# Latent attention with norms by tokens, keys' shared part rotated once, and the output divided with queries on partitions

## The chip, the cores and the metric

The kernel is one program on one core of a Trainium2 chip. The time is device microseconds of one execution, and a kernel's time is the median of several. A profile is one further execution with the hardware profiler on. PE is the TensorEngine, ACT the ScalarEngine, DVE the VectorEngine, POOL GpSimd; SP only issues transfers.

## The reference, cut to what matters

The whole computes two transformer blocks of two layers each. The change lies in one stage, the latent attention (MLA) of the first block's first layer, over 256 context and 512 latent tokens (768, kept as 512 latent and then 256 context), in float32:

```python
def mla_heads(z, q_norm_g, w_uq, kv_norm_g, w_ukv, qn_g, kn_g, ang):
    cq, ckv, kr = z[..., :256], z[..., 256:384], z[..., 384:]      # 256, 128, 32 wide
    q = (rmsnorm(cq, q_norm_g) @ w_uq).reshape(b, t, 8, 96)
    kv = (rmsnorm(ckv, kv_norm_g) @ w_ukv).reshape(b, t, 8, 64 + 64)
    k = concatenate([kv[..., :64], broadcast(kr, 8 heads)], axis=-1)
    v = kv[..., 64:]
    q, k = rmsnorm(q, qn_g), rmsnorm(k, kn_g)                      # over the 96 of each head
    if ang is not None:                                            # latent tokens only
        q = concatenate([q[..., :64], apply_rotary(q[..., 64:], ang)], axis=-1)
        k = concatenate([k[..., :64], apply_rotary(k[..., 64:], ang)], axis=-1)
    return q, k, v

p = softmax(q @ k.T * 96 ** -0.5)      # latent queries: all 768 keys; context queries: context keys
out = p @ v
```

`rmsnorm(x, g)` is `x * rsqrt(mean(x * x) + 1e-6) * g`. After it come a retention over the same input, an output projection and the rest of the network.

## The kernel before, in words

Every engine runs its own program in order, and semaphores tie them together. `PLAN_TICKETS` deals PSUM's eight banks out to the steps in program order: PE claims a ticket's bank (`claim`: it must have been drained the time before), fills it (`fill`), and a reader waits (`filled`) and drains it (`drained`); `emptied` waits for a ticket's drain. `PLAN_BLOCKS` deals the slots of `ring`, which holds weights, and says after which ticket a slot may be loaded anew. SP issues all weight loads in one fixed order, each behind the wait for its slot: `w_in0`, `uq`, `ukv`, twelve `ada_w` halves, four `w_in` blocks for the retention, then, with no wait, 40 copies of later weights (`weights_kept`, `gate_weights`), then `w_out`.

Activations lie with channels on partitions and the 768 tokens along the free side, in two parts of 512 and 256 (`TBS`).

**The stem.** PE multiplies `w_in0` by the input (`z_kv`, `z_q0`, `z_q1`, `z_kr`, L2800). ACT squares and copies each bank; PE sums squares over channels by a product with a matrix of ones (L812), which gives each sum on all partitions; ACT takes roots, DVE inverts 128x512 and 128x256 of them (L855) and scales `cqT` and `ckvT` (L856). `v_tok` holds the values of all heads with tokens on partitions, one product of 128x512 for each of six token tiles (L2810).

**The loop.** `mla_order` yields (step, number) for PE, ACT and DVE alike. Step number n from 0 to 47 is head n // 6 and query tile n % 6; four tiles are latent (768 keys), two are context (256 keys). Steps for n: `scores` n (L2859), `scale` n-1, `turn` n-2 (L2865), `out` n-3 (L2874). DVE takes the maximum (L2072, one for each bank), ACT the exponential with its sum (L1614), DVE divides the probabilities by the sum (L2085), PE turns them so that keys are on partitions, DVE and ACT copy the turned tiles (L2091, L1626), and PE multiplies `v_tok` (64 columns of weights) by them (128 moving columns), with the result as 64 channels x 128 queries; DVE copies it to `mixT` (L2095).

In between, the next head is prepared: `proj` (query L2831 and key L2836 projections, each copied and squared by ACT, the shared `krT` again for each head, L1590 to L1597), `nsum` (ones-products of queries and keys, L2843, and on ACT `Identity`, `Ln` and later `Exp` and `Square`, L824 to L833), `norm` (DVE: a Newton step, L840, L841, and the scaling, L2054) and `rot` (product with the rotation matrix, L2850, and three DVE operations on 32 partitions, L2062 to L2065), the last three for queries and keys apart. `ada`, `adarow`, `adacol` make a piece of the modulation vectors for later layers, one per head (L731, L738, L745). `stay_awake` (L799) issues products of the identity whose result nobody reads.

Names: `qh`, `kh` are the queries and keys of a head (two buffers), `prob_of` three buffers of probabilities, `probT` two of turned ones, `stat` small columns, P = 128, NL = 512, NC = 256, NT = 768, QK = 96, NOPE = 64, H_A = 8.

## Time and profile before

| | us |
|---|---|
| median of 3 runs (lowest, highest) | 3968.12 (3956.37, 3973.16) |
| the profiled execution | 3971.91 |
| its span | 3969.8 |
| PE busy | 3438.6 (87%) |
| DVE busy | 2098.2 (53%) |
| POOL busy | 1103.5 (28%) |
| ACT busy | 1010.4 (25%) |
| mean granted TensorE clock | 0.943 of full speed |

Times are from the span's start. In the stretches below the attention's stem runs from 45.42 to 127.90 us, its loop from 127.90 to 404.60. A busy share is a mean over stages; in a stage, what PE waits for and how its groups follow one another says what a change is worth there. A float32 matmul appears as two records, a transpose as one. The distance between two groups' starts is their pace; the durations of neighbouring groups overlap a little.

### The profile page before, as it was taken

What the parts mean: (1) busy time and instruction counts of PE and PEld (TensorE: products, weight loads), DVE (VectorE), ACT (ScalarE), POOL (GpSimd) and SP (SyncE); (2) the same over time, 40 slices, a digit from 0 to 9 for tenths busy, and PEclk for the clock granted to TensorE, in tenths of its full rate; (3) what the DMA queues carried; (4) which work ended last, traced back from release to release, by engine and by line L of the source; (5) the groups of instructions that cost most, each with busy time, mean ns of one, the idle gap of its engine ahead of it and who ended that gap; (6) DMA issues with size and microseconds to landing.
All of it is one profiled execution on the core that took longest, in us unless ns stands there. A gap on an engine that the chain in (4) does not pass through costs nothing.

```text
span 3969.8 us, 47914 instructions
## 1 busy us (share of the span) xinstructions
PE 3438.6 (87%) x17905; PEld 2225.1 (56%) x17905; DVE 2098.2 (53%) x4783; ACT 1010.4 (25%) x2338; POOL 1103.5 (28%) x1281
## 2 busy tenths in 40 slices
PE   7888999999999989999999999988677897655655
PEld 4555554555555568788878887765454554211111
DVE  3667036462222258511254246788788445666764
ACT  3665114300000032210162221115432222112212
POOL 0000000254322200000000026654746663333332
PEclk9998999999999999999999999999888999877788
DMA  5325993998787324589521349998969999999998
GB/s 199 128 98 177 330 333 98 255 324 274 219 249 232 120 111 160 189 292 361 181 105 65 128 179 406 412 408 331 332 203 370 388 383 387 421 421 391 422 421 344
DMA packets 337280, 1076.52 MB, mean 271 GB/s; under 512 B 22728, under 2 KB 101012, under 8 KB 292148
## 3 DMA queue, kind: packets, MB, share of 16 engines
q1 hardware_dynamic: 222688, 508.04, 37.5%
q0 software_dynamic: 113968, 565.16, 36.3%
q8 instruction: 126, 2.06, 0.2%
q14 instruction: 78, 0.64, 0.0%
q10 hardware_dynamic: 420, 0.62, 0.0%
HBM read 1045.43 MB, written 236.98 MB: 323 GB/s over the span
## 4 chain that ended last, share of the span: by engine, by line
PE 60%; DVE 17%; DMA 10%; ACT 6%; issue 4%; POOL 2%; another core or an unknown queue 1%; SPq 0%; DVEq 0%; ACTq 0%; POOLq 0%
PE bank L973 22%; PE bank L3169 7%; DMA arena<-expert_rows,arena 5%; PE bank L3395 4%; DVE ring L2708 3%; PE bank L2902 3%; PE bank L3136 3%; DMA ring<-expert_rows,arena 3%; DMA arena<-in_peer_v,arena 2%; PE bank L2968 2%; DVE arena L2708 1%; PE bank L3099 1%; DVE arena L2602 1%; PE bank L2800 1%
## 5 line engine op out<-in xcount | busy, mean ns | idle before, releaser
L3395 PE MATMUL bank<-arena 64*64 64x512 f32 x2520 | 391.3, 697 | 149.9 <-ACT arena L2002 120.5
L973 PE MATMUL bank<-hT,ring 128*128 128x256 f32 (+1 forms) x1536 | 445.5, 452 | 1.9 <-ACT hT L866 1.9
L973 PE MATMUL bank<-arena,ring 128*128 128x256 f32 (+1 forms) x1536 | 442.1, 450 | 0.0
L973 PEld LDWEIGHTS bank<-hT,ring 128*128 128x128 f32 x1536 | 292.7, 191 | 153.4 <-issue 122.4
L973 PEld LDWEIGHTS bank<-arena,ring 128*128 128x128 f32 x1536 | 291.8, 190 | 148.9 <-issue 121.5
L3169 PE MATMUL bank<-hT,ring 128*128 128x256 f32 x1536 | 358.8, 391 | 12.2 <-DVE hT L2424 6.3
L3395 PE MATMUL bank<-ring,arena 64*64 64x512 f32 x1256 | 235.0, 775 | 147.3 <-ACT arena L2002 144.3
L1489 POOL DMA_INDIRECT ring<-in_peer_u,arena x256 | 277.5, 1084 | 220.0 <-DVE ring L2708 106.3
L3169 PEld LDWEIGHTS bank<-hT,ring 128*128 128x128 f32 x1536 | 295.5, 196 | 76.7 <-issue 34.0
L2708 DVE SCALAR_TENSOR_TENSOR ring<-ring,xT 128x1024 f32<-128x1024 f32 x256 | 309.2, 1220 | 30.9 <-DMA ring<-in_peer_u,arena 27.5
L1531 POOL DMA_INDIRECT arena<-in_peer_v,arena x240 | 268.7, 1120 | 181.0 <-issue 59.7
L3395 PEld LDWEIGHTS bank<-arena 64*64 64x64 f32 x2520 | 99.6, 149 | 361.4 <-ACT arena L2002 171.4
L2002 ACT ACTIVATE arena<-arena,rstd 128x64 f32<-128x64 f32 x472 | 141.3, 339 | 423.5 <-DVE rstd L2754 380.5
L2708 DVE SCALAR_TENSOR_TENSOR ring<-ring,bank 128x1024 f32<-128x1024 f32 x141 | 171.8, 1220 | 103.6 <-DMA ring<-expert_rows,arena 99.5
L985 ACT ACTIVATE arena<-bank 128x512 f32<-128x512 f32 (+1 forms) x96 | 43.6, 455 | 713.9 <-PE bank L973 713.9
L1005 DVE SCALAR_TENSOR_TENSOR xT<-bank,modT,xT 128x512 f32<-128x512 f32 (+1 forms) x96 | 54.7, 572 | 317.4 <-PE bank L973 317.3
L3395 PEld LDWEIGHTS bank<-ring,arena 64*64 64x64 f32 x1256 | 57.3, 160 | 290.1 <-ACT arena L2002 220.5
L997 DVE TENSOR_TENSOR arena<-arena 128x512 f32<-128x512 f32 (+1 forms) x96 | 55.9, 590 | 278.6 <-ACT arena L985 277.9
L1508 POOL DMA_INDIRECT ring<-expert_rows,arena x141 | 133.9, 949 | 241.4 <-PE bank L3395 211.6
L785 POOL TENSOR_TENSOR hT<-hT 128x256 f32<-128x256 f32 (+1 forms) x30 | 34.7, 1156 | 582.5 <-ACT hT L1907 261.1
L2708 DVE SCALAR_TENSOR_TENSOR arena<-arena,bank 128x1024 f32<-128x1024 f32 x115 | 140.1, 1220 | 76.1 <-DMA arena<-expert_rows,arena 74.7
L1508 POOL DMA_INDIRECT arena<-expert_rows,arena x115 | 109.0, 948 | 170.9 <-PE bank L3395 149.0
(572 smaller groups left out, 5594.9 us busy)
## 6 DMA issues: line engine op xcount, KB each, us to landing
expert_rows<-in_peer_u SPq DMA_DIRECT2D x32, 2048.0 KB, 20.4
expert_rows<-in_peer_v SPq DMA_DIRECT2D x32, 2048.0 KB, 21.7
ring<-in_mlp_w SPq DMA_DIRECT2D x32, 2048.0 KB, 10.9
ring<-in_ada_w SPq DMA_DIRECT2D x24, 2048.0 KB, 10.5
late_weights<-in_mlp_w SPq DMA_DIRECT2D x32, 1024.0 KB, 14.3
ring<-late_weights SPq DMA_DIRECT2D x32, 1024.0 KB
ring<-weights_kept SPq DMA_DIRECT2D x32, 1024.0 KB
s_store<-arena POOLq DMA_DIRECT2D x8, 2816.0 KB, 9.8
```

The lines of the kernel that those rows point to most:

```text
L973: last = pe.matmul(bank[:, 0:hi - lo], w[:, k, m * P:(m + 1) * P], x[:, k, lo:hi], start=(k == 0), stop=(k == 7))
L997: dve.tensor_tensor(hid[:, m, lo:hi], hid[:, m, lo:hi], hid[:, m, lo:hi], ALU.mult)\
L1489: pool.indirect_dma_start(u_row[u % ERING], None, I["peer_u_2"][0], bass.IndirectOffsetOnAxis(idxs[:, u // EXPERTS, u % EXPERTS:u % EXPERT ...
L1508: pool.indirect_dma_start(both_rows[i % F_SLOTS], None, expert_rows, bass.IndirectOffsetOnAxis(idxs[:, u // EXPERTS, u % EXPERTS:u % EXPER ...
L1531: pool.indirect_dma_start(v_row[v_slot(v)], None, I["peer_v_2"][0], bass.IndirectOffsetOnAxis(idxs[:, v // EXPERTS, v % EXPERTS:v % EXPERT ...
L2002: act.activation(diag[:, d % V_SLOTS, :], eye2, ACT.Copy, scale=acts[:, d % (AGROUP * ACT_GROUPS):d % (AGROUP * ACT_GROUPS) + 1]).then_inc ...
L2708: dve.scalar_tensor_tensor(row, row, 1.0, h_tok[u // EXPERTS], ALU.mult, ALU.mult, accum_out=dots[:, u % 64:u % 64 + 1]).then_inc(S("u_use ...
L2902: last = pe.matmul(bank[:, 0:hi - lo], w[:, k, m * P:(m + 1) * P], hT[:, k, lo:hi], start=(k == 0), stop=(k == KD - 1))
L2968: last = pe.matmul(bank[:, 0:hi - lo], w[:, k, m * P:(m + 1) * P], mixT[:, k, lo:hi], start=(k == 0), stop=(k == 7))
L3136: last = pe.matmul(bank[:, 0:HALF], w[:, k, n % 2 * P:n % 2 * P + P], y, start=(k == 0), stop=(k == KD - 1))
L3169: last = pe.matmul(bank[:, first:first + HALF], w[:, k, c:c + P], y, start=(k == 0), stop=(k == KD - 1))
L3395: last = pe.matmul(banks[2 * r + n][QUADS[r if y == 0 else 1 - r], :], diag[QUADS[r], (v + y) % V_SLOTS, :], v_part(v + y)[QUADS[r], 512 * ...
```

## The change

**Norms with tokens on partitions.** The sum of squares of a head's 96 query or 96 key channels is no longer made by ones-products for each head. Before the loop, PE multiplies once more with tokens on partitions: all heads' key parts (`ksq`, six banks of 128x512) and all heads' queries (`qsq`, twelve banks of 128x480 and 128x288). ACT squares them, DVE sums over each head's channels, so that one root of 128x48 holds all heads and tokens. The norms of `cq` and `ckv` go the same way: 12 and 12 products with one column of ones give sums per token (`kvsum`, `qsum`). The gains of `cq` and `ckv` are applied by ACT's copy, before the products. Values are scaled in their copy (`v_tok`).

**Keys.** Their shared 32 channels are rotated once (`krrot`), turned to tokens on partitions (`krtok`), and DVE writes all heads' keys, scaled, into `keys_tok` (`kmul`, two multiplications for each token tile). In the loop a head's keys are six transposes (`kturn`), copied by ACT with the gain.

**Queries** are projected as before, copied with the gain and rotated; they aren't scaled. The root of a query's norm goes into the exponential's scale and the maximum's factor, which are columns with queries on partitions (`q_pos`, `q_neg`).

**Output.** The probabilities are not divided. Turned probabilities are the weights of the output product and 64 channels of `v_tok` move, so that the result has queries on partitions; DVE divides it there into `att_tok` (L2144 of the new kernel), and after two heads six transposes bring it to `mixT` (`mturn`, four times).

**Banks.** `scores` take a pair of banks, 0 and 1 or 2 and 3 by turns, `turn`, `proj`, `kturn` and `mturn` all the pair 4 and 5, `out`, `rot`, `ada` and `adacol` by turns 6 and 7. A pair is read by one instruction of 768 columns. Maxima, exponentials and the copy of the turned tiles, now ACT's alone, are one instruction each. All `stay_awake` in this stage but the first are gone. `uq`'s slot is free after `kturn7`, where it was after a part of `proj7`. Before the retention's products PE now waits for the last `mturn` to be copied.

The core of the diff (removed lines left out where they are told above):

```diff
 def mla_order():
+    yield from (("proj", 0), ("qsq", 0), ("kturn", 0), ("rot", 0), ("ada", 0), ("adarow", 0))
+    for n in range(6 * H_A + 5):
...
-        for lag, step in ((1, "scale"), (2, "turn"), (3, "out")):
+        for lag, step in ((2, "turn"), (3, "out")):
...
+        if n >= 15 and n % 12 == 3:
+            yield "mturn", (n - 15) // 12
...
+        if h < H_A and n % 6 < 3:
+            yield ("proj", "kturn", "rot")[n % 6], h
...
+def mla_tickets():
...
+        if step == "qsq":
+            yield "qsq", 12, (0, 1, 2, 3, 6, 7)
+        elif step == "scores":
+            yield f"scores{n}", 1, (2 * (n % 2),)
+        elif step in ("turn", "proj", "kturn", "mturn"):
+            yield f"{step}{n}", 1, (4,)
+        elif step != "adarow":
+            yield f"{step}{n}", 1, (6 + odd,)
+            odd = 1 - odd
...
+    ("z_kv", 2), ("z_kr", 2),
+    ("ksq", 6), ("kvsum", 1),
+    ("z_q0", 2),
+    ("krrot", 1), ("v_tok", 6),
+    ("z_q1", 2),
+    ("krtok", 1), ("kmul", 6), ("qsum", 1),
+    *mla_tickets(),
...
-    ("uq", 1, lambda j: (f"proj{H_A - 1}", 1), (1,)),
-    ("ukv", 1, lambda j: (f"proj{H_A - 1}", 3), (2,)),
+    ("uq", 1, lambda j: (f"kturn{H_A - 1}", 0), (1,)),
+    ("ukv", 1, lambda j: ("kturn2", 0), (2,)),
...
+        def turn_kept(act, n):
+
+            t = ticket0[f"turn{n}"]
+            filled(act, t)
+            tiles = slice(0, 6) if n % 6 < 4 else slice(4, 6)
+            w = P * (tiles.stop - tiles.start)
+            drained(act.activation(probT[:, n % 2, tiles, :], pair_of(t)[:, 0:w].rearrange("p (t n) -> p t n", n=P), ACT.Copy), t)
...
+                if step == "adarow":
+                    if n:
+                        filled(act, ticket0[f"adacol{n - 1}"])
+                    ada_keep(act, ticket0[f"ada{n}"], ada_rows_mla)
+                    continue
...
+                elif step == "kturn":
+                    filled(act, t0)
+                    drained(act.activation(kh[0:QK, n % 2, :], pair_of(t0)[0:QK, 0:NT], ACT.Copy, scale=small[0:QK, 4:5]), t0)
+                elif step == "scores" or step == "turn" and n >= 6 * H_A - 2:
+                    if step == "scores" and n >= 2:
+                        turn_kept(act, n - 2)
...
                     act.wait_ge(S("score_max"), n + 1)
...
+                    drained(act.activation(prob_of[n % 3][:, keys], pair_of(t0)[:, 0:keys.stop - keys.start], ACT.Exp,
+                                           bias=stat[:, n % 4, 3:4], scale=q_pos[:, 8 * (n % 6) + n // 6:8 * (n % 6) + n // 6 + 1],
+                                           accum_out=stat[:, n % 4, 4:5]), t0)
...
+                elif step == "out":
...
+                    emptied(dve, ticket0[f"scores{n}"])
+                    dve_step(dve, dve.reciprocal(st[:, 6:7], st[:, 4:5]))
                     bank = filled(dve, t0)
+                    drained(dve.tensor_scalar(att_tok[:, h // 2 % 2, n % 6, HEADROWS[h]], bank[:, 0:V_DIM], st[:, 6:7], None, ALU.mult), t0)
...
+            pe.wait_ge(S("kr_rotated"), 1)
+            bank = claim(pe, ticket0["krtok"])
             for t in range(6):
+                last = pe.transpose(bank[:, ROPE * t:ROPE * t + ROPE], krT[NOPE:QK, t * P:(t + 1) * P], ident[NOPE:QK, NOPE:QK])
+            fill(last, ticket0["krtok"])
+            values("kmul", 0)
...
+                elif step == "kturn":
+                    if n == 0:
+                        for t in range(6):
+                            emptied(pe, ticket0["kmul"] + t)
+                    for t in range(6):
+                        last = pe.transpose(pair_of(t0)[0:QK, t * P:(t + 1) * P], keys_tok[t][:, n, :], ident[:, :])
+                    fill(last, t0)
...
                     for t in tiles:
-                        last = pe.matmul(bank[HEADROWS[h], 0:P], v_tok[:, t, h * 64:(h + 1) * 64], probT[:, n % 2, t, :],
+                        last = pe.matmul(bank[:, 0:V_DIM], probT[:, n % 2, t, :], v_tok[:, t, h * V_DIM:(h + 1) * V_DIM],
                                          start=(t == tiles[0]), stop=(t == 5))
                     fill(last, t0)
+            for last in (f"scores{6 * H_A - 2}", f"scores{6 * H_A - 1}", f"mturn{H_A // 2 - 1}"):
+                emptied(pe, ticket0[last])
```

PE in the stem, behind the second pair of input products (line numbers are each kernel's own, `ring` and `arena` are tiles). Before:

```order
L2800 MATMUL bank<-hT,ring 32x512 x8
L2800 MATMUL bank<-hT,ring 32x256 x8
L812 MATMUL bank<-arena,ones 128x512 x2
L812 MATMUL bank<-arena,ones 128x256 x2
L2810 MATMUL bank<-ring,arena 128x512 x6
L799 MATMUL bank<-ident 128x128 x9
L2831 MATMUL bank<-arena,ring 96x512 x2
L2831 MATMUL bank<-arena,ring 96x256 x2
L2836 MATMUL bank<-arena,ring 64x512
L2836 MATMUL bank<-arena,ring 64x256
L799 MATMUL bank<-ident 128x128 x9
L2843 MATMUL bank<-arena,ones 96x512
```

and now:

```order
L2873 MATMUL bank<-arena 32x512
L2845 MATMUL bank<-ring,arena 128x512 x6
L2857 MATMUL bank<-hT,ring 128x512 x8
L2857 MATMUL bank<-hT,ring 128x256 x8
L2878 MATMUL bank<-ident,arena 128x32 x6
L2845 MATMUL bank<-ring,arena 128x512 x6
L2887 MATMUL bank<-ones,arena 128x1 x12
L2915 MATMUL bank<-arena,ring 96x512 x2
L2915 MATMUL bank<-arena,ring 96x256 x2
L2899 MATMUL bank<-ring,arena 128x480 x2
L2899 MATMUL bank<-ring,arena 128x288 x2
```

The sums over channels (L812) are gone; `krrot` (L2873), `v_tok` and `kmul` (both L2845), `krtok` (L2878), `qsum` (L2887), the first `proj` (L2915) and the first banks of `qsq` (L2899) stand there. `ksq` and `kvsum` come ahead of it.

PE in the loop, around the preparation of the third head. Before, from `proj2` on:

```order
L2831 MATMUL bank<-arena,ring 96x512 x2
L2831 MATMUL bank<-arena,ring 96x256 x2
L2836 MATMUL bank<-arena,ring 64x512
L2836 MATMUL bank<-arena,ring 64x256
L2859 MATMUL bank<-arena 128x512
L2859 MATMUL bank<-arena 128x256
L2865 MATMUL bank<-ident,arena 128x128 x2
L2874 MATMUL bank<-arena 64x128 x2
L799 MATMUL bank<-ident 128x128 x3
L2843 MATMUL bank<-arena,ones 96x512
L2843 MATMUL bank<-arena,ones 96x256
L2843 MATMUL bank<-arena,ones 96x512
```

and now, from `proj3` on, where the pattern is full:

```order
L2915 MATMUL bank<-arena,ring 96x512 x2
L2915 MATMUL bank<-arena,ring 96x256 x2
L2934 MATMUL bank<-arena 128x512
L2934 MATMUL bank<-arena 128x256
L2940 MATMUL bank<-ident,arena 128x128 x2
L2951 MATMUL bank<-arena 128x64 x2
L2923 MATMUL bank<-ident,arena 96x128 x4
L2923 MATMUL bank<-ident,ring 96x128 x2
L2934 MATMUL bank<-arena 128x512
L2934 MATMUL bank<-arena 128x256
L2940 MATMUL bank<-ident,arena 128x128 x6
L2951 MATMUL bank<-arena 128x64 x2
```

The key projection, the stay-awake records and the ones-products are gone; the key turn (L2923) follows the output product of the second step, and the output product (L2951) has 64 columns where it had 128.

ACT in the loop, from an exponential on, before (the first rows of a head's norm):

```order
L1614 ACTIVATE arena,stat<-bank,stat 128x256
L824 ACTIVATE arena<-bank,small 96x512
L825 ACT_TABLE_LOAD
L825 ACTIVATE arena<-bank,small 96x512
L824 ACTIVATE arena<-bank,small 96x256
L825 ACTIVATE arena<-bank,small 96x256
L824 ACTIVATE arena<-bank,small 96x512
L825 ACTIVATE arena<-bank,small 96x512
L824 ACTIVATE arena<-bank,small 96x256
L825 ACTIVATE arena<-bank,small 96x256
L829 ACT_TABLE_LOAD
L829 ACTIVATE arena<-arena 96x768
```

and now:

```order
L1652 ACTIVATE arena,stat<-bank,stat,rstd 128x768
L1640 ACTIVATE arena<-bank,small 96x768
L882 ACTIVATE arena<-bank 128x256
L1652 ACTIVATE arena,stat<-bank,stat,rstd 128x768
L1643 ACTIVATE arena<-bank,small 96x768
L882 ACTIVATE arena<-bank 128x768
L1652 ACTIVATE arena,stat<-bank,stat,rstd 128x768
L882 ACTIVATE arena<-bank 128x768
L1652 ACTIVATE arena,stat<-bank,stat,rstd 128x768
```

The table loads and the norm's activations are gone; exponentials (L1652) alternate with copies of turned tiles (L882), with a query copy (L1640) and a key copy (L1643) in between.

## Rows read from the trace of the kernel before

**Rows 1.** Windows: busy time of each engine, granted clock and DMA share by stretch.

```profile
45.42:127.90 82.48, 77.77 (x324) 42.20 (x325) 31.99 (x40) 33.56 (x63) 0.00 (x0) 0.96 0.26 93
127.90:404.60 276.70, 238.93 (x1375) 149.56 (x1375) 191.56 (x471) 169.90 (x396) 0.00 (x0) 0.94 0.40 138
404.60:1423.00 1018.40, 1011.35 (x3235) 573.43 (x3234) 347.85 (x639) 133.69 (x239) 255.84 (x442) 1.00 0.76 240
```

**Rows 2.** Groups by line, the loop, PE's transposes: busy, mean ns | idle before.

```profile
L2865 PE MATMUL bank<-ident,arena 128*128 128x128 f32 x224 | 36.4, 291 | 32.5 <-ACT arena L1614 17.4 <-DVE arena L2085 10.3 <-ACT rstd L738 4.7
```

**Rows 3.** Timeline of PE, stem and first step: start, duration, line, count.

```profile
45.42 22.21 PE L2800 MATMUL bank<-hT,ring 128*128 128x512 f32 x64 [0.55 <-ACT hT L866]
...
68.76 20.92 PE L2800 MATMUL bank<-hT,ring 128*128 128x512 f32 x64
...
92.30 5.31 PE L2810 MATMUL bank<-ring,arena 128*128 128x512 f32 x12
97.44 2.17 PE L799 MATMUL bank<-ident 128*128 128x128 f32 x18
100.51 2.82 PE L2831 MATMUL bank<-arena,ring 128*96 128x512 f32 x8 [0.89 <-DVE arena L856]
103.26 1.50 PE L2836 MATMUL bank<-arena,ring 128*64 128x512 f32 x4
...
107.76 2.82 PE L2843 MATMUL bank<-arena,ones 96*96 96x512 f32 x8 [0.80 <-ACT arena L1597]
110.52 3.63 PE L731 MATMUL bank<-ring,silu_c 128*2 128x256 f32 x64
...
127.90 1.56 PE L2859 MATMUL bank<-arena 96*128 96x512 f32 x4
129.29 0.38 PE L745 MATMUL bank<-ident,rstd 128*128 128x128 f32 x2
```

**Rows 4.** Timeline of PE, the last head.

```profile
373.57 0.59 PE L2859 MATMUL bank<-arena 96*128 96x256 f32 x2
374.00 0.82 PE L2865 MATMUL bank<-ident,arena 128*128 128x128 f32 x6
374.75 1.52 PE L2874 MATMUL bank<-arena 128*64 128x128 f32 x12
376.21 1.10 PE L2850 MATMUL bank<-arena 96*96 96x512 f32 x2
377.14 0.59 PE L2859 MATMUL bank<-arena 96*128 96x256 f32 x2
379.89 1.54 PE L2865 MATMUL bank<-ident,arena 128*128 128x128 f32 x6 [2.15 <-DVE arena L2085]
381.36 2.34 PE L2874 MATMUL bank<-arena 128*64 128x128 f32 x12
```

**Rows 5.** Timeline of PE, a product with eight moving columns.

```profile
1975.34 3.63 PE L3184 MATMUL bank<-blk,hT 128*128 128x8 f32 x32
1978.83 0.46 PE L3169 MATMUL bank<-hT,ring 128*128 128x256 f32 x1
```

**Rows 6.** Groups by line and shape, ACT and DVE in the loop.

```profile
L1614 ACT ACTIVATE arena<-bank,stat 128x256 f32<-128x256 f32 x48 | 22.4, 467 | 66.4 <-DVE stat L2075 66.4
L1614 ACT ACTIVATE arena<-bank,stat 128x512 f32<-128x512 f32 x32 | 21.9, 683 | 40.7 <-DVE stat L2075 40.5
...
L1614 ACT ACTIVATION_READ_ACCUMULATOR arena<-bank,stat 128x1 f32 x80 | 15.6, 194 | 0.0
L833 ACT ACTIVATE arena<-arena 96x768 f32<-96x768 f32 x14 | 11.8, 843 | 0.4
...
L2072 DVE TENSOR_REDUCE stat<-bank 128x1 f32<-128x512 f32 x32 | 22.0, 687 | 53.9 <-PE bank L2859 53.6
```

**Rows 7.** SP's waits, 404.6 to 1423: us in total, times, longest.

```profile
SPq L645 <- PE bank L2968: 115.2, 2, 90.0
```

**Rows 8.** SP's timeline: the copies behind the retention's weight blocks.

```profile
354.41 43.32 SPq L1260 DMA_DIRECT2D weights_kept<-in_w_in  x12
```

367 lines of the change are left out of this document (190 added, 177 removed).

## The prediction

> **What bounds the kernel now.** I read the page first: PE is the busiest engine, and nearly full in all slices up to the middle. So time goes by TensorE's program order, and a stage is worth what it takes there. The table of stretches then gives the attention's two parts [rows 1]: the stem (the products of `w_in0`, the norms and the first head's preparation) from 45.42 to 127.90 us, 82.5 us, and the loop (48 steps, eight heads of six query tiles) from 127.90 to 404.60, 276.7 us, of which PE is busy 238.9 at a mean granted clock of 0.94. The groups by line show who holds it up: nearly all idle time stands before its transposes (L2865), 32.5 us, for ACT's exponential 17.4, for DVE's division of the probabilities 10.3 and for ada's rows 4.7 [rows 2]. ACT is late because a head's norm puts between exponentials four activations of 0.84 us, four of 0.68 and four of 0.47 (as long as the exponentials' two shapes) and two table loads [rows 6], some 10 us.
>
> At full clock the loop's own work can be added up. A matmul is two records. I take the distance from a group's start to the next start, or, where no start follows, the duration less the 0.07 by which groups overlap. From the stem and the first step [rows 3]: latent scores 1.39 us (127.90 to 129.29), a query projection 2.75 (100.51 to 103.26), a key projection 1.43 (its 1.50 less 0.07), a head's ones-products 2.76 (107.76 to 110.52), ada's products 3.56, ada's turn 0.24 with its overlap off, a stay-awake record 0.12. From the last head [rows 4]: context scores 0.43, six transposes 0.75, an output product of 12 records 1.46 or 0.122 a record, a rotation 0.93. With the loop's counts (8 heads of 4 latent and 2 context steps, 6 and 2 tiles each; seven heads prepared; five adas): 32 x 1.39 + 16 x 0.43 = 51.4; 224 transposes x 0.125 = 28.0; 448 output records x 0.122 = 54.5; 7 x 2.75 = 19.3; 7 x 1.43 = 10.0; 7 x 2.76 = 19.3; 14 x 0.93 = 13.0; 42 x 0.12 = 5.1; 5 x 3.56 = 17.8; 6 x 0.24 = 1.4. Together 219.8. Idle is 276.7 - 238.9 = 37.8, so 19.1 us are left for stretches at 1.2 GHz, which follow waits: after the 2.15 us before 379.89, an output product takes 2.34 us in place of 1.52 [rows 4]. A microsecond of waiting thus costs 1.5.
>
> **The loop, part by part.** Gone are the ones-products (19.3), the key projections (10.0), half the rotations (6.5) and the stay-awakes (5.1). Seven key turns of six transposes come in, 7 x 0.75 = 5.3, and four turns of the output, 4 x 0.75 = 3.0. Scores, turns of the probabilities, query projections and ada stay.
>
> The output product swaps its operands: the weights are now 128 columns of `probT`, the moving side 64 columns of values, in as many records (448). By moving columns a record would halve, 0.061. But a product later in the trace has 128 x 128 weights and 8 moving columns, and its 32 records start over 3.49 us, 0.109 each [rows 5]: below some width records get no shorter. The bounds are 0.061 and 0.122; I take 0.109, since that row has the new form's weights: 448 x 0.109 = 48.8, not 54.5.
>
> The Trainium skill, page "TensorE: Matmul & The Clock Gate", section "LDWEIGHTS (loading the stationary operand)", gives a weight load's time as its column count over 1.2, in ns. By it 128 columns cost 107 ns a record whatever streams past, and the swap saves little; the trace agrees (0.109).
>
> New full-clock sum: 51.4 + 28.0 + 48.8 + 19.3 + 5.3 + 6.5 + 3.0 + 17.8 + 1.4 = 181.5 us.
>
> ACT and DVE no longer bound anything. The norm's work on ACT goes, table loads included. For 768 columns I extend the shapes of 512 and 256 [rows 6]: an exponential 0.68 + 0.22 = 0.90 and 0.19 to read its sum, a copy of turned tiles about as long, a maximum 0.69 x 1.5 = 1.03 at most. A head then takes on ACT 4 x 1.09 + 2 x 0.66 for exponentials, 4 x 0.9 + 2 x 0.47 for turned tiles, 2 x 0.9 for query and key and about 1.5 for ada, 13.5 us, and on DVE about 11 (maxima 5, rotation 2, divisions and factors 4). PE has 22.7 (181.5 / 8). The division of probabilities that PE waited for leaves the path: the quotient is formed behind the output product.
>
> What is late next I find by following one head. After the scores of step n, maximum and factor take 1.3 us, and the exponential ends 2.9 us after the scores, because ACT first copies turn n-2. PE needs it only at turn n, two steps of 3.4 us later. Two places don't fit. At n % 6 = 1 the key turn takes the one bank pair that the turns of the probabilities use, and ACT drains it behind an exponential: turn n-1 of the next step waits about 0.7 us, 7 times, 5. And `ada_keep` (1.5 us of ACT) stands behind the exponential of n % 6 = 3, while the output product of the next step wants ada's bank (two banks take turns): about 1.3 us, 5 times, 6.5. The pipe's start costs 2; at its end the last output, its division, the last turn and ACT's copy of it are one chain before `z_rq`, for which PE now waits: 4. Together 17.5 us of waits, and at 0.5 more for the clock, 9. **Loop: 181.5 + 17.5 + 9 = 208 us, 69 less.** Bounds: 160 with output records of 0.061 and no waits; 240 with records of 0.122 and twice the waits.
>
> **The stem.** The two pairs of input products now take 22.1 and 20.8 us [rows 3], 42.9, after the change as before. Added are three sets of six 512-column products, `ksq`, `v_tok` (which was there) and `kmul`, 5.14 each (92.30 to 97.44, [rows 3]): 15.4; the token sums, 48 records at 0.109, 5.2; the keys' rotation 0.93 and its turn 0.75; `qsq`, six token tiles over 768 columns twice, as much as six query projections, 16.5; the first projection 2.75, key turn 0.75, rotation 0.93 and ada 3.56. These are 46.8. Behind each new wait of PE all the rest of its program is queued, so I followed them: the keys' roots are due before `kmul` and `kr_rotated` before its turn, and `z_q0`, `v_tok` and `z_q1`, 27 us, cover both; the queries' roots, about 4 us of DVE and ACT, lie beside turn, rotation and ada (5.2 us). I allow 1 us. First scores at 45.4 + 42.9 + 46.8 + 1 = 136, against 127.9: **8 us more**. Low end 0, if one-column products are cheaper; high end 16, if DVE's six reductions and twelve multiplications show.
>
> **Behind the attention.** From 404.6 to 1423 PE is busy 1011.4 of 1018.4 us [rows 1], and up to 2300 none of its waits names a DMA. The copies of kept weights that SP issues behind the third `w_in` block start at 354.41 [rows 8], 50 us before the loop's end. That block now waits for the last key turn at step 37, some 33 us before the end, so they come 17 us later against PE. SP afterwards waits up to 90 us for PE at one load [rows 7], which swallows 17, and the block itself is wanted only after `z_rq` and `z_rk`. So I let the whole gain through.
>
> **Sum.** 69 - 8 = 61 us. The profiled execution took 3971.91 us (span 3969.8); 3910.9 for its like. The median shown is 3968.12, 3.8 lower: 3907.
>
> **Rivals.**
> Outputs halve: at 0.061 a record the loop loses 21.5 us more. For it: moving columns set the pace of the wide forms here. Against it: the 8-column row. 3907 - 21 = 3886. Chance 0.08.
>
> A faster pipe: the two bank conflicts don't arise and no stretch falls to 1.2 GHz: 11.5 + 9 = 20 us less, 3887. For it: each is near a microsecond by my count; against it: today's pipe waits at just such places. Chance 0.15.
>
> More waits: without stay-awakes and with a single bank pair PE idles as much as now, 37.8 us and 19 for the clock, so the loop is 238 and the time 3907 + 30 = 3937. For it: the last head, with no norm in it, still waits 2.15 us for DVE [rows 4]; against it: that was the division, which goes. Chance 0.12.
>
> Given back later: the 17 us of later copies reach PE. For it: their queue is full from 354 on; against it: the 90 us. 3924. Chance 0.06.
>
> Slower: the single pair for turns and ACT's strict order make each step one chain: scores 1.39, maximum 1.3, exponential 1.1, turn 0.75, copy 0.9, output 1.3, so 6.7 us for a latent and about 3 for a context step. A head is then 4 x 6.7 + 2 x 3 + 8.0 of preparation = 40.8, the loop 326, and the time 3968 + 50 + 8 = 4026. It decides from 33.6 us a head on, (276.7 - 8) / 8. Against it: scores alternate over two bank pairs and run two steps ahead. Chance 0.02.
>
> The forecast itself has 0.57, within 3896 and 3920. For 8 in 10 over all cases I take 3880 to 3940, which holds the first four rivals. A measurement of this kernel tells about 0.5%, 20 us, from no change: faster 0.95 (all but the last rival and the far ends of two others), within 0.5% 0.03, slower 0.02.
>
> **What would show it.** The profile after should have the first scores near 136 us and `z_rq` near 344; no table load on ACT between the first exponential and the loop's end; output records 0.109 apart; under 20 us of waits of PE in the loop, among them the transposes after a key turn and the outputs after ada; a clock above 0.94 there; and the stretches from `z_rq` on as long as before. I am wrong if the loop stays above 240 us, if the stem grows by over 16, or if a later stretch lengthens by over 10.

## The result: 72 us faster, and where the trace shows them

The changed kernel takes 3897.74 us (median of 4 runs, 3896.71 to 3900.24); the kernel before 3970.27 us (median of 4 runs, 3956.37 to 3973.16; the three known ahead of the prediction and one more). The ratio is 0.9825 with a 95% interval of 0.9801 to 0.9849. Forecast were 3907 us within 3880 and 3940, so sign, size and range hold; the time is 9 us below the forecast, the gain 72.5 us where 61 were forecast. The profiled execution took 3898.42 us, with a span of 3895.5.

First the two parts of the attention and the stretch behind them, from the changed kernel's table of stretches. The columns are length, busy time and instruction count of PE, PEld, DVE, ACT and POOL, then granted clock, DMA share and GB/s.

```profile
45.58:138.89 93.31, 93.31 (x349) 48.51 (x349) 28.67 (x58) 30.97 (x59) 0.00 (x0) 0.96 0.10 37
138.89:333.10 194.21, 180.23 (x1305) 129.45 (x1301) 79.47 (x219) 98.32 (x187) 0.00 (x0) 0.99 0.54 190
333.10:1351.50 1018.40, 1011.25 (x3231) 572.18 (x3232) 347.10 (x635) 133.34 (x238) 255.65 (x442) 1.00 0.78 245
```

Against [rows 1] the stem grows from 82.5 to 93.3 us (10.8 more; forecast 8), the loop falls from 276.7 to 194.2 us (82.5 less; forecast 69), and 1018.40 us counted from `z_rq` on still hold the same work: 1011.25 us of PE, where it was 1011.35. To the end of the span it is 3562.4 us, where it was 3565.2; these 2.8 us were not forecast, and no run explains them. In the loop DVE's busy time falls from 191.6 to 79.5 us, ACT's from 169.9 to 98.3, and the granted clock goes from 0.94 to 0.99.

The groups by line show the loop's PE again; they answer to [rows 2]. Columns: busy time, mean ns of one record, and behind the second bar the idle time before them with what ended it.

```profile
L2951 PE MATMUL bank<-arena 128*128 128x64 f32 x448 | 55.9, 271 | 3.8 <-ACT rstd L752 3.6 <-ACT arena L882 0.2
L2940 PE MATMUL bank<-ident,arena 128*128 128x128 f32 x224 | 32.9, 275 | 5.4 <-ACT arena L1643 3.4 <-ACT arena L1657 1.9
```

The transposes of the probabilities (now L2940) had 32.5 us of idle time before them and have 5.4. No row names the exponential (L1652) any more, and the division (L2144) only once, for 0.5 us before the last turn of the output. PE idles 14.0 us in all (194.21 - 180.23), and its waits say for what (total, times, longest):

```profile
PE bank L2951 <- ACT rstd L752: 3.6, 5, 0.8
PE bank L2940 <- ACT arena L1643: 3.4, 7, 1.3
PE bank L745 <- DMA ring<-in_ada_w: 2.5, 1, 2.5
PE bank L2940 <- ACT arena L1657: 1.9, 3, 1.0
PE bank L2981 <- issue: 1.1, 1, 1.1
PE bank L2945 <- DVE arena L2144: 0.5, 1, 0.5
```

The first is `ada_keep` before the next output product, 5 times, the second the drain of the key turn from the shared bank pair, 7 times: both places that the prediction named. The third it did not name. The last head, from PE's timeline, gives the paces of the new forms (start, duration, line, count), beside [rows 4]:

```profile
317.01 1.51 PE L2934 MATMUL bank<-arena 96*128 96x512 f32 x4
318.36 0.82 PE L2940 MATMUL bank<-ident,arena 128*128 128x128 f32 x6
...
322.70 0.65 PE L2934 MATMUL bank<-arena 96*128 96x256 f32 x2
323.19 0.82 PE L2940 MATMUL bank<-ident,arena 128*128 128x128 f32 x6
323.84 1.45 PE L2951 MATMUL bank<-arena 128*128 128x64 f32 x12
325.13 0.65 PE L2934 MATMUL bank<-arena 96*128 96x256 f32 x2
```

From start to start: latent scores 1.35 us (317.01 to 318.36), context scores 0.49, six transposes 0.65, an output product 1.29 for 12 records, 0.1075 each.

The stem, from the same view, beside [rows 3]:

```profile
73.10 0.28 PE L2868 MATMUL bank<-ones,arena 128*128 128x1 f32 x2
...
76.71 12.28 PE L2857 MATMUL bank<-hT,ring 128*128 128x512 f32 x32
88.93 1.04 PE L2873 MATMUL bank<-arena 32*32 32x512 f32 x2
...
111.31 2.73 PE L2887 MATMUL bank<-ones,arena 128*128 128x1 f32 x24
113.90 4.49 PE L2915 MATMUL bank<-arena,ring 128*96 128x512 f32 x8
118.23 15.64 PE L2899 MATMUL bank<-ring,arena 128*128 128x480 f32 x48
133.71 0.60 PE L2923 MATMUL bank<-ident,arena 128*96 128x128 f32 x4
```

PE never waits in the stem (93.31 us busy of 93.31), yet the granted clock is 0.96. The two slow places stand directly behind the two sets of one-column sums: `z_q0` takes 12.2 us (76.71 to 88.93) and the first projection 4.33 us (113.90 to 118.23), for 10.5 and 2.6 at full clock. The granted clock over these two stretches is 0.86 and 0.61, and 1.00 over the stretches between and behind them.

ACT and DVE, groups by line and shape, beside [rows 6]:

```profile
L1652 ACT ACTIVATE arena<-bank,stat,rstd 128x768 f32<-128x768 f32 x32 | 31.6, 989 | 12.1 <-DVE stat L2133 12.1
L882 ACT ACTIVATE arena<-bank 128x768 f32<-128x768 f32 x32 | 25.9, 810 | 53.0 <-PE bank L2940 52.9
L1652 ACT ACTIVATION_READ_ACCUMULATOR arena<-bank,stat,rstd 128x1 f32 x48 | 9.5, 198 | 0.0
...
L1652 ACT ACT_TABLE_LOAD x1 | 1.3, 1283 | 0.0
```

```profile
L2132 DVE TENSOR_REDUCE stat<-bank 128x1 f32<-128x768 f32 x32 | 30.6, 958 | 61.7 <-PE bank L2934 61.7
```

One table load is left, before the first exponential. ACT now waits mostly for PE (53 us before the copies of turned tiles), where it had waited mostly for DVE's maxima (107 us before the exponentials, now 12).

SP's timeline, beside [rows 8], shows the transfers that the prediction followed.

```profile
259.61 40.05 SPq L659 DMA_DIRECT2D ring<-in_w_in  x4
299.70 44.95 SPq L1291 DMA_DIRECT2D weights_kept<-in_w_in  x12
...
544.22 19.75 SPq L659 DMA_DIRECT2D ring<-in_ada_w  x2
633.93 0.37 SPq L659 DMA_DIRECT2D ring<-in_mlp_w  x1
```

The kept copies start 33.4 us before the loop's end (333.10 - 299.70), where they had 50.2. SP still stands still for some 70 us later on (564 to 633.93), so the 17 us are swallowed and nothing is given back.

### The profile page after: what moved, and what is told of

Read it like the earlier page. It is cut to its first block, busy times and chain, and to the rows that moved or that the text cites. A ratio compares the mean times of both kernels' runs of the same rounds, so it can differ in the third digit from the quotient of the medians.

```text
span 3895.5 us, 47385 instructions
## 1 busy us (share of the span) xinstructions
PE 3408.8 (88%) x17855; PEld 2216.6 (57%) x17855; DVE 1983.0 (51%) x4548; ACT 935.9 (24%) x2125; POOL 1110.5 (29%) x1281
## 4 chain that ended last, share of the span: by engine, by line
PE 66%; DVE 15%; DMA 10%; ACT 5%; issue 3%; another core or an unknown queue 1%; POOL 0%; SPq 0%; DVEq 0%; ACTq 0%; POOLq 0%
PE bank L1004 23%; PE bank L3248 9%; PE bank L3474 5%; DMA arena<-expert_rows,arena 4%; DVE ring L2757 4%; DMA ring<-expert_rows,arena 4%; PE bank L2981 3%; PE bank L3215 3%; PE bank L3047 2%; PE bank L3178 1%; DVE arena L2757 1%; DVE arena L2651 1%; PE bank L2857 1%; DMA arena<-in_peer_v,arena 1%; PE bank L2973 1%
## 5 line engine op out<-in xcount | busy, mean ns | idle before, releaser
L3474 PE MATMUL bank<-arena 64*64 64x512 f32 x2520 | 399.4, 704 | 133.0 <-ACT arena L2032 116.3
L1520 POOL DMA_INDIRECT ring<-in_peer_u,arena x256 | 277.4, 1084 | 208.8 <-DVE ring L2757 94.6
L1562 POOL DMA_INDIRECT arena<-in_peer_v,arena x240 | 276.6, 1153 | 180.8 <-PE bank L3474 62.5
L2757 DVE SCALAR_TENSOR_TENSOR ring<-ring,xT 128x1024 f32<-128x1024 f32 x256 | 309.0, 1220 | 22.8 <-DMA ring<-in_peer_u,arena 17.4
## 6 DMA issues: line engine op xcount, KB each, us to landing
ring<-in_ada_w SPq DMA_DIRECT2D x24, 2048.0 KB, 10.5
late_weights<-in_mlp_w SPq DMA_DIRECT2D x32, 1024.0 KB, 14.4
```

Of the source, the lines that this page charges most:

```text
L1520: pool.indirect_dma_start(u_row[u % ERING], None, I["peer_u_2"][0], bass.IndirectOffsetOnAxis(idxs[:, u // EXPERTS, u % EXPERTS:u % EXPERT ...
L1562: pool.indirect_dma_start(v_row[v_slot(v)], None, I["peer_v_2"][0], bass.IndirectOffsetOnAxis(idxs[:, v // EXPERTS, v % EXPERTS:v % EXPERT ...
L2757: dve.scalar_tensor_tensor(row, row, 1.0, h_tok[u // EXPERTS], ALU.mult, ALU.mult, accum_out=dots[:, u % 64:u % 64 + 1]).then_inc(S("u_use ...
L3474: last = pe.matmul(banks[2 * r + n][QUADS[r if y == 0 else 1 - r], :], diag[QUADS[r], (v + y) % V_SLOTS, :], v_part(v + y)[QUADS[r], 512 * ...
```

## The experiments

Four kernels start from the kernel before, seven from the changed one. Unless it is said otherwise each was run once, with a profile, and is judged by its stretches: stem (from `z_kv`'s start to the first scores) and loop (from there to `z_rq`). The total of one run says little: those of the kernel before lie between 3956 and 3974 us. A stretch moves less, but it moves too. The changed kernel, profiled again, had a stem of 93.30 and a loop of 194.47 us; yet three kernels below with that stem unaltered had 93.31, 93.30 and 91.61, and two with that loop unaltered 192.80 and 192.74. The loops differ mainly in one place, the second ada's product, behind the same wait for its weights (the changed kernel, then one of the two):

```profile
152.46 5.10 PE L745 MATMUL bank<-ring,silu_c 128*2 128x256 f32 x64 [2.52 <-DMA ring<-in_ada_w]
```

```profile
146.57 3.63 PE L745 MATMUL bank<-ring,silu_c 128*2 128x256 f32 x64 [2.50 <-DMA ring<-in_ada_w]
```

So a difference of under 2 us between two loops, or two stems, shows an edit's effect only where a wait or a pace in the trace accounts for it.

### What the old loop's time was: norms, division, stay-awakes

The three kernels below leave out parts of the computation of the kernel before. Without the division (the probabilities go on undivided):

```diff
-                    dve_step(dve, dve.reciprocal(st[:, 6:7], st[:, 4:5]))
-                    keys = slice(0, NT) if two else KEYS[1]
-                    dve.tensor_scalar(prob_of[n % 3][:, keys], ..., st[:, 6:7], None, ALU.mult)\
-                       .then_inc(S("prob_ready"), 1)
+                    dve.reciprocal(st[:, 6:7], st[:, 4:5]).then_inc(S("prob_ready"), 1)
```

> The kernel before, with the division of the probabilities left out (the output isn't the reference's). Theory: in the loop 10.3 us of PE's waits stand before transposes for that division, and each waited microsecond costs half again in clock, so the loop falls from 276.7 to about 262 us and the wait of L2865 for DVE to under 2. Rival: another wait of the same pipe (the exponential, the banks) ends at the same place, and the loop stays above 273.

Without the heads' norms (queries and keys are used unnormed, and squares, ones-products, roots and the stay-awake records ahead of the ones-products are gone; the key projection stays):

```diff
-    for step in ("nsum", "ada", "norm", "rot"):
+    for step in ("ada", "rot"):
...
-            for at, step, m in ((0, "proj", h), (1, "nsum", 2 * h), ..., (2, "norm", 2 * h),
-                                (3, "norm", 2 * h + 1), (3, "rot", 2 * h), (4, "rot", 2 * h + 1)):
+            for at, step, m in ((0, "proj", h), (3, "rot", 2 * h), (4, "rot", 2 * h + 1)):
```

> The kernel before, with the per-head norms left out: no squares, no ones-products (and the stay-awakes ahead of them), no roots, no Newton step, no scaling; the projections, the copies and both rotations stay. Theory: PE loses 19.3 + 5.1 us of work, its 17.4 us of waits for the exponential behind the norm's activations and the 3.0 for rotated keys, with the clock's half on top: the loop falls from 276.7 to about 222. Rival: the waits belong to the pipe and not to the norm, only the work goes: about 252.

Without both:

> The kernel before with both left out, the division and the per-head norms. Theory: what either frees adds up, loop about 207 us, PE's waits under 8 us in all, granted clock 0.98 or more. Rival: the pipe of the kernel before has waits of its own of some 20 us, loop above 225.

Measured: loop 267.2 us without the division, 208.8 without the norms, 203.0 without both (276.7 with all). The waits of the first, then the stretches of the second and third:

```profile
PE bank L2862 <- ACT arena L1614: 17.4, 7, 4.6
PE bank L2862 <- ACT rstd L738: 6.4, 4, 1.6
PE bank L2856 <- DVE arena L2065: 3.4, 5, 0.7
PE bank L2862 <- DVE stat L2083: 3.0, 5, 1.2
```

```profile
117.84:326.59 208.75, 202.28 (x1276) 126.27 (x1277) 148.80 (x415) 88.65 (x264) 0.00 (x0) 0.99 0.49 171
```

```profile
117.67:320.64 202.97, 199.37 (x1276) 126.47 (x1277) 124.52 (x367) 88.47 (x264) 0.00 (x0) 1.00 0.49 172
```

The division alone is worth 9.5 us: the wait for DVE before the transposes falls from 10.3 to 3.0, and 17.4 us for the exponential stand untouched. That is two thirds of what the theory gave (262 us, and under 2 of waits for DVE); it ends between theory and rival, since the exponential's wait stays and ada's rows grow from 4.7 to 6.4. The norms alone are worth 68 us, more than either theory gave (222 was the lower). Ones-products and stay-awakes are 24.4 us of this (19.3 + 5.1); 31.3 are idle time, 37.8 us before and 6.5 now (208.75 - 202.28), and the rest is the clock, 0.99 for 0.94. The stem, where the first head's norm stands, falls as well, from 82.5 to 71.8 us. With the norms gone the division is worth only 5.8 us, not 9.5: the gains overlap. Norm and division stood in one queue on DVE, which would make them share a bottleneck, but no run separates that queue from ACT's. So the old loop's waits were nearly all the norm's, those for the division included in part. The third kernel bears its theory out (203.0 us, 3.6 of waits, a clock of 1.00), and it tests the method of adding paces: the prediction's full-clock work without ones-products and stay-awakes is 219.8 - 19.3 - 5.1 = 195.4 us, and this loop shows 199.4 us of PE. The sum is 4.0 us short, so the prediction put 4 us of the old loop's work down to the clock.

The stay-awake records went with the change. What they did in the kernel before, with all of them taken out of the order around the norm:

```diff
-                        stay_awake(pe, t0, 9)
...
-                    if n % 2 == 0:
-                        stay_awake(pe, t0, 9 if n == 0 else 3)
...
-                    if n < 2:
-                        stay_awake(pe, t0, (15, 2)[n])
...
-                    if n == 0:
-                        stay_awake(pe, t0, 7)
```

> The kernel before, the stay-awake products of this stage left out, all but the first. Theory: in the loop they are 5.1 us of PE that in part lie in waits, and what they save of the clock is small: loop within 5 us of 276.7. In the stem they fill waits: PE idles instead, and the first head's products run at 1.2 GHz, the stem 2 to 6 us longer. Rival: they hold the clock up in the loop too; without them the clock falls well below 0.94 there and the loop takes 10 us more or longer, so that the change would have gained less if its own waits hadn't gone.

Measured: stem 86.4 us (3.9 more, clock 0.87), loop 281.6 us (4.9 more, clock 0.92 where it was 0.94). Both lie within the theory's ranges, the loop at the upper end. PE's waits in the loop grow by 3.0 us to 40.8: those before the ones-products, where three stay-awake products had stood, from 0.8 to 5.8. So they had filled waits, and without them PE waits in their place and at a lower clock. Whether any would help the changed loop, with 14 us of waits at 0.99, was not tried.

### Where the quotient is formed

The changed kernel with the division back on the probabilities, as a step of its own before the transposes, and a plain copy behind the output product:

```diff
-        for lag, step in ((2, "turn"), (3, "out")):
+        for lag, step in ((1, "scale"), (2, "turn"), (3, "out")):
...
+                    dve.tensor_scalar(prob_of[n % 3][:, keys], ..., st[:, 6:7], None, ALU.mult)\
+                       .then_inc(S("prob_ready"), 1)
...
-                    dve_step(dve, dve.reciprocal(st[:, 6:7], st[:, 4:5]))
-                    drained(dve.tensor_scalar(att_tok[...], bank[:, 0:V_DIM], st[:, 6:7], None, ALU.mult), t0)
+                    drained(dve.tensor_copy(att_tok[...], bank[:, 0:V_DIM]), t0)
```

> The changed kernel with one part undone: DVE divides the 768 or 256 probabilities again before they are turned, and the output is only copied. Theory: the pipe of the changed kernel has two steps (6.8 us) between the scores and the turn, and max, exponential and division together take some 4 us of them, so little of the division shows: loop 194.2 to about 198 us, waits of PE's transposes for DVE up to 4. Rival: the division stands in PE's way as in the kernel before, where leaving it out gave 9.5 us: loop 204 or more.

Measured: loop 195.3 us, 1.1 more. DVE is busy 100.3 us for 79.5, and PE waits for it twice, 0.8 us in all, which is most of the 1.1. The direction is right, the size a quarter of what I had put. Once DVE is free of the norm it has room for the division in its old place: dividing later is not what makes this kernel fast.

### Queries on partitions

The changed kernel with the output product's old operand order (64 columns of values as weights, 128 of `probT` streaming, undivided, into `mixT` without the four turns of the output; the division is left out):

```diff
-        if n >= 15 and n % 12 == 3:
-            yield "mturn", (n - 15) // 12
...
-                        last = pe.matmul(bank[:, 0:V_DIM], probT[:, n % 2, t, :], v_tok[...],
+                        last = pe.matmul(bank[HEADROWS[h], 0:P], v_tok[...], probT[:, n % 2, t, :],
```

> The changed kernel with the output product turned back: 64 columns of values are the weights and 128 columns of turned probabilities move; the division is left out (so the output isn't the reference's), DVE copies, and the four last turns are gone. Theory: a record takes 0.122 us in place of 0.1075, 448 x 0.0145 = 6.5 us, and the transposes beside it go back from 0.65 to 0.75 for six, 3.7, while the last turns save 2.6: loop 194.2 to about 202. Rival: moving columns set a record's time, then the swap was worth 448 x 0.05 = 24, and the loop goes to 216 or more. Second rival: the transposes' pace has to do with the bank claims and not with the neighbour's 64 columns: they stay at 0.65, loop about 198.

Measured: loop 197.9 us, 3.7 more. PE's timeline of one latent step of this kernel, with the transposes now L2934 and the output L2945:

```profile
236.50 1.56 PE L2928 MATMUL bank<-arena 96*128 96x512 f32 x4
237.89 0.82 PE L2934 MATMUL bank<-ident,arena 128*128 128x128 f32 x6
238.64 1.52 PE L2945 MATMUL bank<-arena 128*64 128x128 f32 x12
240.09 0.70 PE L2928 MATMUL bank<-arena 96*128 96x256 f32 x2
```

Scores take 1.39 us again, six transposes 0.75 (237.89 to 238.64), the product 1.45. In the changed kernel they take 1.35, 0.65 and 1.29. Where the 0.10 us at six transposes stands, single records show (the last ones of such a group and the first of the product; this kernel, then the changed one):

```profile
238.44 0.27 PE L2934 MATMUL bank<-ident,arena 128*128 128x128 f32 x1
238.64 0.32 PE L2945 MATMUL bank<-arena 128*64 128x128 f32 x1
```

```profile
323.62 0.38 PE L2940 MATMUL bank<-ident,arena 128*128 128x128 f32 x2
323.84 0.22 PE L2951 MATMUL bank<-arena 128*128 128x64 f32 x1
```

Here six transposes start between 237.89 and 238.44, 0.11 us apart, and the product 0.20 after the last. In the changed kernel they start 0.11 apart as well, from 323.19 on (the two in the row are the fifth and sixth), and the product 0.11 after the last. So the transposes themselves are as quick in both; the border to the product costs 0.09 more in the old form. Groups of two show the same, 0.31 us for 0.22. The bank claims are the same in both, so this comes with the form of the product behind the transposes (64 columns of weights, 128 streaming); which of its two sides does it isn't told apart. The rival of the bank claims falls by this, though the loop's value is the one that it gave. The swap is worth 448 x 0.0142 (0.1217 - 0.1075) = 6.4 us in outputs and some 4.5 at the borders of 48 groups; it costs 4 x 0.65 = 2.6 for the turns of the output and 5.2 of idle time (14.0 against 197.9 - 189.1 = 8.8), most of it at those turns and in the tail before `z_rq`. This leaves 3.1 of the 3.7 us. The rest isn't resolved: other groups moved by some hundredths too, as the scores did.

### One read over two banks

The changed kernel with its maximum and its exponential of 768 columns in two parts, 512 and 256, as before the change; maxima and sums are combined by one more small operation each:

```diff
-                    drained(act.activation(prob_of[n % 3][:, keys], pair_of(t0)[:, 0:NT], ACT.Exp, ...), t0)
+                        act.activation(prob_of[n % 3][:, 0:NL], pair_of(t0)[:, 0:NL], ACT.Exp, ...)
+                        drained(act.activation(prob_of[n % 3][:, NL:NT], pair_of(t0)[:, NL:NT], ACT.Exp, ...), t0)
...
-                    dve_step(dve, dve.reduce_max(st[:, 0:1], pair_of(t0)[:, 0:NT], AX_X))
+                        dve.reduce_max(st[:, 1:2], pair_of(t0)[:, NL:NT], AX_X)
+                        dve_step(dve, dve.reduce_max(st[:, 0:1], pair_of(t0)[:, 0:NL], AX_X))
+                        dve_step(dve, dve.tensor_tensor(st[:, 0:1], st[:, 0:1], st[:, 1:2], ALU.max))
```

> The changed kernel with the exponential and the maximum of a latent step in two instructions again, 512 and 256 columns, each with its sum or maximum, which DVE puts together. Theory: ACT and DVE have room (98 and 79 us busy of 194), the chain from scores to turn has two steps, so one instruction or two decides nothing: loop 194 to 197 us. Rival: reading a bank pair at once is part of what made the pipe free of waits: loop above 200.

My theory fell and its rival holds: the loop takes 208.6 us, 14.4 more. The stretch and the waits of this kernel:

```profile
137.32:345.91 208.59, 187.24 (x1304) 135.76 (x1301) 91.94 (x315) 109.29 (x251) 0.00 (x0) 0.96 0.53 184
```

```profile
PE bank L2953 <- ACT arena L1643: 7.6, 7, 1.9
PE bank L2964 <- ACT rstd L752: 5.0, 5, 1.3
```

I had reasoned that ACT, busy 98 of 194 us, has room for 11 us more. On average it has; at the places where it drains a shared bank right behind an exponential it has none: the key turn's wait grows from 3.4 to 7.6 us, ada's from 3.6 to 5.0. The edit splits DVE's maximum as well, 79.5 us busy and now 91.9, and both engines take part. At the third head's key turn the copy of the turned keys starts 2.82 us after the maximum (174.47 to 177.29), in the changed kernel 2.23 (173.93 to 176.16). Of these 0.59 us, 0.25 lie before the exponential, in DVE's chain, and 0.34 in the exponential; PE's wait there is 0.94 us for 0.35, all 0.59 more. Idle time is 21.4 us for 14.0, and PE's own work takes 7.0 us longer at a clock of 0.96 for 0.99. So 7.4 us more of waits came with 14.4 us more of loop, in one run.

### What the one-column sums do to the clock

The changed kernel with the sums over tokens made 40 (keys) and 80 (queries) columns wide instead of one, the sums themselves unchanged:

```diff
-                        pe.matmul(bank[:, t:t + 1], ckv_sq[...], ones[:, 0:1], start=True, stop=True)
-                        last = pe.matmul(bank[:, 6 + t:7 + t], kr_sq[...], ones[NOPE:QK, 0:1], ...)
+                        pe.matmul(bank[:, 40 * t:40 * t + 40], ckv_sq[...], ones[:, 0:40], start=True, stop=True)
+                        last = pe.matmul(bank[:, 240 + 40 * t:280 + 40 * t], kr_sq[...], ones[NOPE:QK, 0:40], ...)
...
-                    last = pe.matmul(bank[:, t:t + 1], sqs[...], ones[:, 0:1], ...)
+                    last = pe.matmul(bank[:, 80 * t:80 * t + 80], sqs[...], ones[:, 0:80], ...)
```

> The changed kernel with the token sums made with 40 (keys) and 80 (queries) moving columns of ones in place of one, same weights, same number of products. Theory: the granted clock, 0.60 over the projection behind the 24 one-column records and 0.86 over z_q0 behind the others, fell because of those stretches; with wider ones the projection takes 2.6 us in place of 4.3 and z_q0 10.5 in place of 12.2, the stem 93.3 to about 90, and the sums themselves take as long as now. Rival: the clock's fall has another cause (it is as low with the wide sums), stem 93.

Measured: stem 93.6 us, no gain. The projection behind the queries' half takes 2.60 us for 4.33, as in the theory. Behind the keys' half the contrary is seen: its 24 records take 4.47 us for 3.6, at a clock that falls to 0.86 while they still run, and `z_q0` behind them 13.3 us for 12.2. So making them wider did not keep the clock there. The next kernel has half of the keys' sums away instead (the shared part's, so the keys' norm is not the reference's):

```diff
-                        pe.matmul(bank[:, t:t + 1], ckv_sq[...], ones[:, 0:1], start=True, stop=True)
-                        last = pe.matmul(bank[:, 6 + t:7 + t], kr_sq[...], ones[NOPE:QK, 0:1], ...)
+                        last = pe.matmul(bank[:, t:t + 1], ckv_sq[...], ones[:, 0:1], start=True, stop=True)
```

> The changed kernel without the twelve one-column products of the keys' shared part (their sums are taken from the other twelve, so the norm of the keys is not the reference's). In question is why z_q0 behind these sums takes 12.2 us for 10.5. Theory: the low clock follows upon PE having streamed almost nothing for 3.6 us; with half the records the gap is 1.3 us (12 records of 0.107), and z_q0 takes 10.5 to 11.2. Rival: any such products bring it, or it has another cause: z_q0 stays at 12 us. The sums themselves get 2.3 us shorter (3.6 to 1.3) if the switching between 128 and 32 rows costs the 0.15 a record, 1.8 us shorter if the pace stays at 0.15.

PE's timeline of this kernel:

```profile
73.01 1.40 PE L2868 MATMUL bank<-ones,arena 128*128 128x1 f32 x12
74.26 10.57 PE L2857 MATMUL bank<-hT,ring 128*128 128x512 f32 x32
...
107.14 2.73 PE L2886 MATMUL bank<-ones,arena 128*128 128x1 f32 x24
109.73 2.80 PE L2914 MATMUL bank<-arena,ring 128*96 128x512 f32 x8
```

`z_q0` is back at 10.5 us, as the theory has it, and the sums take 1.25 us, 0.104 a record: alternating weights of 128 and of 32 rows made it 0.15. The edit takes out half of the records and the 32-row weights together, so it could not tell which of the two matters. And two more rows speak against the theory itself. The last two lines show the queries' sums as in the changed kernel, 24 records of one column in 2.6 us, with the projection behind them at full clock (109.73 to 112.37, 2.64), where it took 4.33. And the kernel with two reads has the changed kernel's stem unaltered, all 24 of the keys' records among them (73.22 to 76.84), but not the slow `z_q0`:

```profile
76.84 10.59 PE L2870 MATMUL bank<-hT,ring 128*128 128x512 f32 x32
87.36 1.04 PE L2886 MATMUL bank<-arena 32*32 32x512 f32 x2
```

Behind the alternating sums `z_q0` took 12.2 us in five profiles and 10.5 in this one; behind 24 queries' records of one column the projection took 4.0 to 4.3 us in five and 2.64 in one. So with the same records ahead of it a stretch may run at the low level or not, and one run of each edit can't show what either did. That the stem here is 87.5 us, 5.8 less, of which 2.4 are the records, 1.7 `z_q0` and 1.7 the projection, is in its last two terms no proof for the edit; what decides is not settled by these runs. The loop of this kernel and that of the one before it are the two unaltered ones of 192.7 and 192.8 us told of above.

### A version with both remedies

Two edits on the changed kernel: ada's rows are copied right behind their products, one step earlier, and the queries' sums alone are 80 wide.

```diff
-        if h < ADA_IN_MLA and n % 6 in (2, 3, 4):
-            yield ("ada", "adarow", "adacol")[n % 6 - 2], h
+        if h < ADA_IN_MLA and n % 6 == 2:
+            yield "ada", h
+            yield "adarow", h
+        if h < ADA_IN_MLA and n % 6 == 4:
+            yield "adacol", h
```

> The changed kernel with two edits: ada's rows are copied one step earlier, directly behind their products, and the queries' token sums (alone) take 80 columns in place of one. My theory: the 3.6 us of waits before ada's turns on ACT's ada rows (L752) go, with some tenths of clock, so the loop takes 190 to 191 us in place of 194.2; the first projection runs at full clock again and the stem shortens by about 1.7 us. Together 5 us: 3893, 0.13 per cent, at the edge of what five rounds tell. Rival: ACT copies the same rows in any case, and what it does earlier delays an exponential instead, so that the loop stays at 194 and only the stem's 1.7 us come.

It was timed in five rounds, beside the changed kernel unaltered:

> The changed kernel unaltered, as the measure for the other kernels of this call: 3898 us, stem 93.3 us, loop 194.2 us of it.

```profile
138.86:326.54 187.68, 177.43 (x1304) 129.09 (x1301) 79.45 (x219) 98.94 (x187) 0.00 (x0) 1.00 0.56 196
```

The first edit does its work: the wait on ada's rows is gone (idle 10.2 us for 14.0), and the loop takes 187.7 us for 194.2. Of these 6.5 us, 3.7 are waits and 1.5 the second ada's product, which stands behind the same wait for its weights as before and runs at full clock here (3.63 us for 5.10), as it did in the two unaltered loops; against those the loop is 5.0 us shorter. The stem takes 91.6 us for 93.3, all of it in the projection, which also ran at full clock without this edit; whether the wider sums did it is not shown. Against the changed kernel profiled beside it, stem and loop together are 8.5 us shorter, but the whole profiled execution only 6.7 (3892.83 and 3899.50), since what comes ahead of the stem took 1.9 us longer. The medians don't bear even that out: 3891.82 us (3887.79 to 3897.73) against 3892.77 us (3889.52 to 3899.50), ratios to the kernel before of 0.9809 (0.9794 to 0.9823) and 0.9810 (0.9797 to 0.9824). The means of the five differ by 1.8 us, with a standard error of 2.4. Behind the loop the two profiles are equally long (3564.4 us each). The low stretches that come and go could account for some of it, but where the other executions lose time stays open. I don't call this version faster.

## Why the prediction was right, point by point

**What bounds it.** PE's order sets the time, and the sum of paces forecasts it: right, with a sum that comes out a little short. The changed loop's paces come to 175.4 us (32 x 1.345 + 16 x 0.49 for scores, 32 x 0.655 + 16 x 0.22 for transposes, 448 x 0.1075 for outputs, 7 x 2.61 for projections, 7 x 0.70 and 4 x 0.65 for the key and output turns, 7 x 0.98 for rotations, and 19.2 for ada). What the work really takes, the last kernel shows, whose loop has the same records on PE: 177.4 us at a clock of 1.00. So the changed loop is 177.4 us of work, 14.0 of waits and 2.8 for the clock. Forecast were 181.5, 17.5 and 9.

**Output record.** 0.109 was taken between 0.061 and 0.122; it is 0.1075. Moving columns don't set it; the 8-column row [rows 5] was the right neighbour. By the Trainium skill, page "TensorE: Matmul & The Clock Gate", section "LDWEIGHTS (loading the stationary operand)", 128 columns take 107 ns to load; the distance between this trace's records, 107.5 ns, agrees.

**The mis-sized term of the work** is one I had no reason to touch: the transposes, forecast at 28.0 us, now 24.5, and with them the key and output turns, 7.5 for 8.3. I had divided 0.75 us by six, but 0.20 of it is the border to an output product of the old form, which the change itself did away with. These are 4.3 of the 6.1 us between 181.5 and 175.4.

**Waits.** The key turn's (5 forecast, 3.4), ada's (6.5 forecast, 3.6) and the end (4 forecast; 1.1 + 0.5 and the 0.2 before the last output) are where they were put, all smaller. The pipe's start, 2 forecast, shows none. Not foreseen were 1.9 us before transposes for the copy of a turned output (one more user of the same bank pair) and 2.5 us for the second ada's weights: their slot in the ring comes free behind `z_q1`, and SP issues the loads from 105.67 us, 16 us later than before, while the loop starts 11 us later.

**Clock.** 9 us forecast, 2.8 measured, the term furthest off. The rule of 1.5 us a microsecond of waiting had taken 4.0 us of work for clock: with these the old loop's 37.8 us of waits cost 15.1, 1.4 each. In the changed loop it is 1.2 (14.0 and 2.8), and more than half of the 2.8 is the one product behind the wait for weights, which runs slow or not. For single waits the rule fits one case and not the other: 5.0 us for 3.7 in the last kernel, 14.4 for 7.4 in the one with two reads.

**ACT and DVE.** The extended shapes: exponential 0.99 us for 0.90, copy 0.81 for about 0.90, maximum 0.96 for at most 1.03. ACT's head is 98.3 / 8 = 12.3 us for 13.5. They bound nothing as a sum, as forecast; the experiment with two reads shows that both together still do at two places.

**The stem.** 10.8 us for 8. What was mis-sized is the token sums: 5.2 forecast for 48 records at 0.109, measured 6.2, since half of them alternate between weights of 128 and 32 rows (0.15). What follows them was taken at full clock and in this run was not: 1.7 us each for `z_q0` and the projection. `qsq` gave 1.0 back (15.5 for 16.5). No wait at all appeared; I had allowed 1 us.

**Behind.** The whole gain carried through, by the slack that I had named, and 2.8 us more that I had not.

**How good the number is.** The profiled execution is 12.5 us below the 3910.9 forecast for it, and that is the loop, 13.8 below its 208, two thirds of the way to the rival of a faster pipe; the stem's 2.8 more and the 2.8 less behind the attention cancel. The median is only 9.3 below 3907, since the changed kernel's lies 0.7 us under its profiled execution, where I had taken over 3.8. So the mechanism held, and that the number falls into the narrow range of 3896 to 3920, by 2 us, is in part luck.

**The rivals.** Outputs halve: refuted by 0.1075. A faster pipe: partly so, since both conflicts are there but cost 7.0 us together instead of 11.5. More waits: no, 14.0 us. Given back later: no. A chain of 6.7 us a step: no; a latent step goes at 3.3 (1.35 + 0.65 + 1.29).

**Which part of the change did it.** By the kernels from before, norms with their stay-awakes are worth 68 us of loop, and the division's wait 9.5 alone and 5.8 behind them: 73.7 together. The other 8.8 us of the 82.5 are the balance of the keys' path (no key projection, half the rotations; key turns in their place), which has no experiment of its own, and of the swap, 3.7 by its experiment. One edit that the prediction passed over as a mere change of shape, reading both banks in one instruction, is worth 14 us in this loop, in that it takes time out of DVE and ACT just where PE waits for them; it overlaps with the others and can't be added to them.

## What to carry to other kernels

When an operation is taken out of an engine's queue, price the waits that other operations of that queue have caused too, and expect the single gains to overlap: division 9.5 alone, 5.8 after the norms. Judge an engine's slack where it drains a bank that another needs next, not by its share of busy time: 11 us more on ACT and 12 on DVE, one half idle and one more than half, cost 14. Take the pace of a kept operation with the neighbours it will have. And before an edit is credited with a stretch's clock, look at the same stretch in runs without that edit.
